# A two-layer encoder kernel: the piece of projection ahead of the scores in each attention group, and the next layer's constants loaded during the last product

## The reference, cut to what matters

```python
def encoder_trunk(x, p, ...):
    x = layer_norm(x, ln0_g, ln0_b)
    for i in range(DEPTH):                       # DEPTH = 2
        mix = hybrid_mixer(x, w_in[i], q_norm[i], k_norm[i], sink[i], ..., w_out[i], ang1d, ang2d)
        x = layer_norm(ALPHA * x + mix, ln1_g[i], ln1_b[i])
        ffn = conv_glu(x, w_up[i], conv_w[i], conv_b[i], w_down[i])
        gate = jax.nn.sigmoid(x @ w_ple_gate[i] + b_ple_gate[i])
        ple = p[i].astype(x.dtype) @ w_ple[i]
        x = layer_norm(ALPHA * x + ffn + gate * ple, ln2_g[i], ln2_b[i])
    return x

def hybrid_mixer(x, w_in, ...):
    h = x @ w_in                                 # 1024 x 1536: q, k, v of both kinds
    qa, ka, va, qb, kb, vb = jnp.split(h, ...)
    oa = global_axial_attention(...)             # 8 heads, rms-normed q and k, rotary angles
    ob = window_sink_attention(...)              # 8 heads, band of 128, a sink in the softmax
    o = jnp.concatenate([rms_norm(oa, ...), rms_norm(ob, ...)], -1)
    return o @ w_out
```

## Time and profile before

| | |
|---|---|
| median of 3 runs | 1215.49 us (1215.14 to 1216.63) |
| the profiled execution's own time | 1215.36 us |
| its span in the trace | 1213.60 us |
| granted TensorE clock, mean | 0.997 of full speed |
| busy: PE / DVE / ACT / POOL | 1192.3 / 526.7 / 492.4 / 593.9 us |
| chain of work that ended last: share on PE | 93% |
| DMA | 115.68 MB, 95 GB/s mean |

### The profile page before, as it was taken

One profiled execution on the slowest core, in us unless ns is written; L12 is line 12 of the kernel. 1 busy time (PEld: TensorE's weight loads), 2 busy tenths in 40 slices (PEclk: granted clock), 3 DMA queues, 4 the chain that ended last, 5 costly groups with the idle time before them and its releaser, 6 DMA issues.

```text
span 1213.6 us, 17810 instructions
## 1 busy us (share of the span) xinstructions
PE 1192.3 (98%) x5800; PEld 974.2 (80%) x5800; DVE 526.7 (43%) x1098; ACT 492.4 (41%) x899; POOL 593.9 (49%) x342
## 2 busy tenths in 40 slices
PE   7999999999999999999999999999999999999997
PEld 6887778888888888888878777788888888888886
DVE  7777847532122134211477777375211122431108
ACT  3456753344344333323144767433443333332321
POOL 6665844455443444344155756634653444434442
PEclk9999999999999999999999999999999999999999
DMA  6321213344333332222132202433433333222331
GB/s 220 88 74 49 88 45 113 113 130 139 98 92 87 103 104 95 79 97 95 56 90 70 80 27 70 126 116 89 139 104 104 100 90 102 90 85 91 102 104 70
DMA packets 122854, 115.68 MB, mean 95 GB/s; under 512 B 6816, under 2 KB 97952, under 8 KB 122784
## 3 DMA queue, kind: packets, MB, share of 16 engines
q1 hardware_dynamic: 122784, 114.81, 30.7%
HBM read 112.70 MB, written 2.10 MB: 95 GB/s over the span
## 4 chain that ended last, share of the span: by engine, by line
PE 93%; DVE 2%; DVEq 1%; issue 1%; POOL 1%; DMA 1%; ACT 0%; SPq 0%; ACTq 0%
PE ps L1219 28%; PE ps L1221 28%; PE ps L1220 28%; PE ps L1371 3%; PE ps L1385 3%; PE ps L1359 1%; PE ps L1361 1%; PE ps L1342 1%; PE ps L1229 1%; POOL w_lo L537 1%; DMA scratch<-in_ln_b_dram 1%; DVEq L875 0%; DVEq L1202 0%; DVE x L880 0%; POOL ln_r L533 0%
## 5 line engine op out<-in xcount | busy, mean ns | idle before, releaser
L527 POOL TENSOR_TENSOR w_lo<-raw,w_hi 128x1024 fp32r<-128x1024 f32 x192 | 461.7, 2406 | 411.4 <-ACT w_hi L635 411.4
L1219 PE MATMUL ps<-xt_hi,w_hi 128*128 128x512 f32 x704 | 273.9, 389 | 0.0
L1220 PE MATMUL ps<-xt_lo,w_hi 128*128 128x512 f32 x704 | 273.9, 389 | 0.0
L1221 PE MATMUL ps<-xt_hi,w_lo 128*128 128x512 f32 x704 | 273.9, 389 | 0.0
L635 ACT ACTIVATE w_hi<-raw 128x1024 fp32r<-128x1024 f32 x192 | 201.9, 1055 | 132.7 <-PE ps L1221 66.6
L1219 PE MATMUL ps<-w_hi,stat 128*128 128x512 f32 x480 | 188.3, 392 | 0.0
L1220 PE MATMUL ps<-w_lo,stat 128*128 128x512 f32 x480 | 187.1, 390 | 0.0
L1221 PE MATMUL ps<-w_hi,stat 128*128 128x512 f32 x480 | 187.0, 390 | 0.0
L1219 PEld LDWEIGHTS ps<-xt_hi,w_hi 128*128 128x128 f32 x704 | 132.1, 188 | 27.6
L1220 PEld LDWEIGHTS ps<-xt_lo,w_hi 128*128 128x128 f32 x704 | 132.1, 188 | 27.5
L1221 PEld LDWEIGHTS ps<-xt_hi,w_lo 128*128 128x128 f32 x704 | 132.1, 188 | 27.3
(11 more groups left out here) (123 smaller groups left out, 1330.8 us busy)
## 6 DMA issues: line engine op xcount, KB each, us to landing
raw<-in_w_up_dram SPq DMA_DIRECT2D x88, 512.0 KB, 3.8
raw<-in_w_down_dram SPq DMA_DIRECT2D x44, 512.0 KB, 3.2
raw<-in_w_in_dram SPq DMA_DIRECT2D x26, 512.0 KB, 3.8
raw<-in_w_out_dram SPq DMA_DIRECT2D x16, 512.0 KB, 3.8
raw<-in_w_ple_gate_dram SPq DMA_DIRECT2D x16, 512.0 KB, 3.9
scratch<-in_ln_g_dram SPq DMA_DIRECT2D x5, 512.0 KB, 4.5
scratch<-in_ln_b_dram SPq DMA_DIRECT2D x5, 512.0 KB, 6.0
raw<-in_w_ple_dram SPq DMA_DIRECT2D x4, 512.0 KB, 3.7
```

Of the source, the lines that this page charges most:

```text
L527: pool.tensor_tensor(w_lo[:, n, :], raw[:, n % RAW, :], w_hi[:, n, :].bitcast(F32), ALU.subtract).then_inc(w_split.sem, 1)
L1219: pe.matmul(out, a[0], b[0], start=first, stop=False)
L1220: pe.matmul(out, a[0], b[1], start=False, stop=False)
L1221: return pe.matmul(out, a[1], b[0], start=False, stop=last)
```

## The change

Five edits, all inside the layer loop or at its head:

1. In `pe_plan`, `scores(g)` for g from 2 to 31 stands behind the group's piece of projection instead of ahead of it (`scores(1)` stays).
2. `rot(2, t)` moves from g = 6, 10, 14, 18 to g = 7, 11, 15, 19, and the second `p_t` from g = 26 to g = 27, with the copies of both on ACT and DVE one group later; on DVE `mean_squares` moves from the end of its group to right behind the maxima.
3. SP loads the first layer's constants before the loop and the next layer's during the down product, behind the looped part and ahead of the last tiles; the last layer loads the first one's again.
4. DVE makes `rope_a` (`gain_tables`) before the loop and then in each layer before it waits for the down product; ACT's and DVE's waits for constants at the loop's head are gone.
5. `norm_lo(1)` at a layer's end moves behind the norm of tile 3.

```diff
@@ pe_plan
     for g in range(GROUPS + 4):
-        if 0 < g < GROUPS:
-            steps.append(("scores", g))
+        if g == 1:
+            steps.append(("scores", 1))
...
             steps.append(("ple", 0, g - 33))
+        if 1 < g < GROUPS:
+            steps.append(("scores", g))
...
-        if g in (6, 10, 14, 18):
-            steps.append(("rot", 2, (g - 6) // 4))
-        if g in (25, 26):
-            steps.append(("p_t", g - 25))
+        if g in (7, 11, 15, 19):
+            steps.append(("rot", 2, (g - 7) // 4))
+        if g in (25, 27):
+            steps.append(("p_t", (g - 25) // 2))
@@ sync
-                sp.wait_ge(h_done.sem, h_done.at(layer, 0))
...
+            load_constants(0)
...
+                following = (layer + 1) % DEPTH
+                sp.wait_ge(h_done.sem, h_done.at(layer, FT))
+                load_constants(following)
                 for r in range(1, REST):
                     raw_free(DOWN_AT + LOOPED + r)
                     load(DOWN_AT + LOOPED + r, down_source(layer, LOOPED + r), 1)
@@ vector
+            def gain_tables(landed):
+                dve.wait_ge(const_landed.sem, landed)
...
             dve.wait_ge(fixed_landed.sem, 16)
+            gain_tables(64)
             with dve.Fori(0, DEPTH) as layer:
...
-                dve.wait_ge(const_landed.sem, const_landed.at(layer, 64))
...
+                    if g in (15, 23, 31):
+                        mean_squares((g - 15) // 8)
...
+                gain_tables(const_landed.at(layer, 128))
                 for t in range(TT - 1):
                     wait_down(dve, layer, t)
                     norm_sum(t, DOWN_BANK[t], ln_rstd.at(layer, 4 + t + 1), norm_landed.at(layer, 64), down_free)
-                    if t in (1, 2):
-                        norm_lo(t - 1, xt_hi_done.at(layer, 13 + 2 * (t - 1)))
+                    if t == 1:
+                        norm_lo(0, xt_hi_done.at(layer, 13))
...
                 dve.drain().then_inc(down_free.sem, 1)
+                norm_lo(1, xt_hi_done.at(layer, 15))
```

More of the change, by code:

```diff
@@ L431, in _, with load_constants @@
             sp.dma_start(rope_sb[:, :, :, :], rope).then_inc(fixed_landed.sem, 16)
-            with sp.Fori(0, DEPTH) as layer:
-                def raw_free(s):
-                    sp.wait_ge(w_split.sem, w_split.at(layer, s - AHEAD - RAW + 1))
-                sp.wait_ge(h_done.sem, h_done.at(layer, 0))
+            def load_constants(layer):
                 sp.dma_start(cols[:, :], columns[bass.ds(layer, 1)].rearrange("a p n -> (a p) n")).then_inc(const_landed.sem, 16)
@@ L442, in _, with raw_free @@
                 sp.dma_start(sinks[:, :], bcast(sink[bass.ds(layer, 1)].rearrange("a n -> (a n)"))).then_inc(const_landed.sem, 16)
+            load_constants(0)
+            with sp.Fori(0, DEPTH) as layer:
+                def raw_free(s):
+                    sp.wait_ge(w_split.sem, w_split.at(layer, s - AHEAD - RAW + 1))
                 for s in range(AHEAD, UP_AT):
@@ L770, in _ @@
                         qkt_evac(1, 3)
-                    if g in (7, 11, 15, 19):
-                        qkt_evac(2, (g - 7) // 4)
+                    if g in (8, 12, 16, 20):
+                        qkt_evac(2, (g - 8) // 4)
                     if g in (3, 7, 11, 15):
                         win(2, (g - 3) // 4)
-                    if g in (26, 27):
-                        k = g - 26
+                    if g in (26, 28):
+                        k = (g - 26) // 2
                         act.wait_ge(tr_full.sem, tr_full.at(layer, TR["p_t", k] + 1))
@@ L909, in _ @@
                     norm_lo(t - 1, 2 * t - 1)
+            def gain_tables(landed):
+                dve.wait_ge(const_landed.sem, landed)
+                for i in range(2):
+                    g = gains[:, i, :].unsqueeze(1).to_broadcast([P, 2, HD])
+                    gs = (gains[:, i, :].rearrange("p (i b) -> p i b", b=2)[:, :, ::-1].unsqueeze(1)
+                          .to_broadcast([P, 2, HD // 2, 2]))
+                    dve.tensor_tensor(rope_a[:, 2 * i, :, :], rope_sb[:, 0, :, :], g, ALU.mult)
+                    dve.tensor_tensor(rope_a[:, 2 * i + 1, :, :].rearrange("p t (i b) -> p t i b", b=2),
+                                      rope_sb[:, 1, :, :].rearrange("p t (i b) -> p t i b", b=2), gs, ALU.mult)
+                dve.tensor_scalar(neg_sinks[:, :], sinks[:, :], -1.0, None, ALU.mult)
+                dve.drain()
+                dve.tensor_scalar(rope_a[:, 2:4, :, :], rope_a[:, 2:4, :, :], 8.0, None, ALU.mult)
+                dve.drain()
             dve.wait_ge(fixed_landed.sem, 16)
+            gain_tables(64)
             with dve.Fori(0, DEPTH) as layer:
@@ L1103, in glu @@
                     dve.tensor_tensor(dst, dst, ps[:, bank + 1, :], ALU.mult).then_inc(h_done.sem, 1)
-                dve.wait_ge(const_landed.sem, const_landed.at(layer, 64))
-                for i in range(2):
-                    g = gains[:, i, :].unsqueeze(1).to_broadcast([P, 2, HD])
-                    gs = (gains[:, i, :].rearrange("p (i b) -> p i b", b=2)[:, :, ::-1].unsqueeze(1)
-                          .to_broadcast([P, 2, HD // 2, 2]))
-                    dve.tensor_tensor(rope_a[:, 2 * i, :, :], rope_sb[:, 0, :, :], g, ALU.mult)
-                    dve.tensor_tensor(rope_a[:, 2 * i + 1, :, :].rearrange("p t (i b) -> p t i b", b=2),
-                                      rope_sb[:, 1, :, :].rearrange("p t (i b) -> p t i b", b=2), gs, ALU.mult)
-                dve.tensor_scalar(neg_sinks[:, :], sinks[:, :], -1.0, None, ALU.mult)
-                dve.drain()
-                dve.tensor_scalar(rope_a[:, 2:4, :, :], rope_a[:, 2:4, :, :], 8.0, None, ALU.mult)
-                dve.drain()
                 norm_lo(2, xt_hi_done.at(layer, 1))
@@ L1144, in _ @@
                         heads_lo((g - 6) // 2)
-                    if g in (15, 23, 31):
-                        mean_squares((g - 15) // 8)
-                    if g in (26, 27):
-                        k = g - 26
+                    if g in (26, 28):
+                        k = (g - 26) // 2
                         dve.wait_ge(p_hi.sem, p_hi.at(layer, k + 1))
```

6 lines of the change are left out of this document (3 added, 3 removed).

## The result

The changed kernel takes 1219.2 us (median of 20), the kernel before, measured beside it, 1216.3: a ratio of 1.0024 [1.0018, 1.0031]. It is slower by 0.24%, where 1215.9 and no difference were forecast; the median lies 0.2 us above the range. The forecast was counted from a median of three, 1215.49, while the 20 executions of the kernel before lie in two groups, eight from 1214.8 to 1215.5 and twelve from 1216.25 to 1216.85; so 0.8 us of the miss of 3.3 is the base, and 2.5 is the change (+0.4 forecast, +2.9 measured). The profiled execution took 1220.24 us with a span of 1218.4, so 4.88 more than the profiled execution of before.

The account below looks back on a forecast made before the run. PE, busy 98% of the span, was taken to bound the kernel. From 1215.36, +2.4 (attention), -1.2 (seam) and -0.8 (tail) give 1215.8; with the median 0.13 above, 1215.9 us, range 1211.0 to 1219.0.

Parts of the forecast that it names:

- The lead: Attention up to group 30: PE arrives there 2.8 us earlier a layer, between 1.8 and 3.4, as holes vanish.
- The new waits inside the groups: Attention groups: short new waits for DVE's rotate and ACT's later copies, put at 0.6 us, between 0 and 1.6.
- The chain: Groups 30 to 32: dependent steps to outb_half(1)'s second half take 13.18 us against 9.21, 3.97 longer.
- The step that failed: Behind groups 30 to 32: PE's dense work carries the delay through, +2.4 us for both layers (+1.2 to +4.4).
- the signs that the prediction named: Profile after: old attention holes gone, waits under 2 and about 2.5 us at outb_half, seam hole about 3, PE wait near 1.
- The seam: Between the layers: PE may go on earlier after DVE's rotate(0, 0), gain 1.2 us, bounds 2.0 and 0.
- the third rival: Seam: DVE's hole goes with the constants, gain 2.0 instead of 1.2 us, time 1215.1; chance 0.12.
- the two readings weighed: Seam: the jump's 3.19 us count from the issue of norm_lo(1)'s last operation or its end; norm_lo(2) at 620.9 to 621.5.
- The end: Last layer's tail: tile 3's norm and last store come earlier with norm_lo(1) behind, gain 0.8 us (0.5 to 1.2).
- What was to cost nothing: Down product: SP's four added constant loads (bare 1.9 us a layer) and DVE's tables (bare 1.5) are hidden in waits.
- The slower one: Attention rival: new waits in the groups eat the lead and the longer chain is paid in full, 1219.7 us; chance 0.13.
- The kept lead: Attention rival: POOL's slot 21 remainder or last outa does not bind, each layer gives 2.8, 1207.9 us; chance 0.15.

Follow-up runs that it names:

- both_links: Changed kernel with POOL making slot 21's remainder ahead of normalise(30), and outb_half(0) waiting for seven outa, outb_half(1) for the eighth: 1207.5 us.
- old_order: Changed kernel with scores(g) back ahead of the piece of projection in every group, all other edits kept: 1206.6 us.
- fill: Changed kernel with products of zeros in PE's two new waits of each layer, eight ahead of outb_half(0)'s wait, ten between outb_half(1)'s halves: 1215.4 us.
- dve_written_out: Changed kernel with scores ahead of the piece again and DVE's loop over the two layers written out as two copies: 1205.4 us.
- attention_only: Kernel before with the attention's edits alone (scores behind the piece; rot(2), p_t, mean_squares moved); constants, table, norm_lo(1) as before: 1221.8 us.
- rem21_first: Changed kernel with POOL making the remainder of slot 21 ahead of normalise(30) instead of behind it: 1211.1 us.
- s31_ahead: Changed kernel with scores(31) alone put back ahead of its piece, outb_half(0): 1210.1 us.

## Why the prediction was wrong

**The lead: right.** Forecast 2.8 us a layer. In both orders `sumsq(2)` closes group 30. PE reached it 94.45 us after the layer's first scores before and reaches it after 91.42 (160.71 - 69.29), so the lead is 3.03; with the scores ahead it is 3.28 (91.17), where 3.4 was the most that the groups could give. The new waits inside the groups were put at 0.6 and came to 0.25. The other 0.38 by which both_links is behind old_order is the wait left there.

**The chain: right.** Forecast 13.18 us from the start of group 30's piece to the second half of `outb_half(1)`. With the clock at full speed it is 171.84 - 158.70 = 13.14 in fill and 768.26 - 755.09 = 13.17 in layer 1 of after. The wait ahead of `outb_half(0)` was forecast at 1.75 and is 1.62, the other at about 2.5 and is 2.13. By waits alone the forecast was +1.2 a layer, and fill shows +0.98 and +0.97.

**The step that failed** is the sentence that closes this part: "What follows is PE's dense work, so it carries through." It carries the delay through, but not at the usual distance of starts. The pace behind a wait was taken from the earlier trace rows, where no such wait stands ahead, and each wait was weighed by its length alone. The clock's fall adds 1.55 us to a wait of 1.6 to 2.2, and it came three times in the profiled execution: +4.65 that no term and no bound held. With it the forecast's own terms give 1215.8 + 4.65 = 1220.4, and 1220.24 was measured. That this is so close is luck in part: the waits cost 0.45 less than forecast (1.95 for 2.4) and the seam gave 0.45 less (0.75 for 1.2). The upper bounds taken together, 1219.4, hold the median as well, but by a smaller lead and not by a fall. And the signs that the prediction named came out, the places and releasers of both waits, the hole ahead of `norm_lo(2)` and 0.90 us of PE's wait at the seam; none of them asks for the clock.

The trace of before had shown such a fall, at a place that the prediction does not use. At the start PE waits 2.15 us for a weight remainder, and behind it stand these two stretches:

```profile
21.77 0.50 PE L1219 MATMUL ps<-w_hi,xt_hi 128*128 128x512 f32 x1 [2.15 <-POOL w_lo L537]
```

```profile
22.00:24.00 2.00, 2.00 (x6) 1.29 (x5) 1.85 (x5) 0.00 (x0) 2.00 (x1) 0.55 0.31 87
24.00:26.00 2.00, 2.00 (x6) 1.57 (x6) 1.56 (x2) 0.34 (x1) 1.54 (x2) 0.60 0.80 210
```

There it costs next to nothing, since PE, when it is not slowed, waits again soon after: in the profiled execution of after the clock stays at the start, PE waits 0.69 us at 23.88 and 0.84 at 33.60, and the first scores are only 0.17 us earlier. At groups 32 and 33 no such slack follows. The same trace holds the other case, too: behind the 2.12 us at the seam the clock is 1.00. So the forecast could not have been certain of a fall, but it had a row for it, and its upper bound, +4.4 for both layers, should have held up to four falls more.

Single executions of the changed kernel spread from 1216.7 to 1221.6. That they differ in the number of falls would fit the size, but their mean granted clocks bear it out for the two longest at most (0.991 and 0.992); it is 0.995 at 1216.66 and at 1220.39 alike. Where this spread comes from is open.

**The seam: size off.** Forecast -1.2, measured -0.75 after, and -1.2 to -1.9 in the other kernels with all the edits of the seam and the loop as it was. The first half of the step holds, and by more than forecast: the hole behind the jump stays at 3.2 us, it did not go with the constants (the third rival), and it counts from the issue of `norm_lo(1)`. So `norm_lo(2)` starts 3.40 us after the norm of tile 3 (620.86 to 624.26), where the two readings weighed gave 4.0 and 4.6. The second half, 4.65 us from `norm_lo(2)` to the end of `rotate(0, 0)`, does not hold: the hole inside `rotate(0, 0)`, 0.46 at the seam of before, is 1.82 after and 0.46 to 1.36 in the others with the loop. A hole of 0.5 stands at the same place in layer 0 of all ten kernels with the loop, where DVE comes to it without a jump back. Here that of before:

```profile
32.23 0.70 DVE L923 TENSOR_TENSOR ps<-ps,rope_a 128x512 f32<-128x512 f32 x1 [0.49 <-issue]
```

In dve_written_out both layers are without it. So it belongs to the loop; that the part above 0.5 belongs to the jump is likely but not shown, and why its length changes from kernel to kernel is open.

**The end: right.** Forecast -0.8, measured -0.85. **What was to cost nothing** cost nothing: the stretch with the added loads and the table takes 430.19 us and took 430.16.

**The rivals.** The slower one named 1219.7, close to the time, with a mechanism that did not happen: in-group waits that eat the lead. They came to 0.25 us a layer, and none is in the list of waits. The kept lead did not happen here either, but it is what old_order and both_links do, and its 1207.9 is within 1.3 us of both.

## What to carry to other kernels

A wait of a PE-bound kernel has two prices: its length, and the pace of the products behind it. Read the granted clock by short stretches behind every wait of more than 1.5 us, the longest in the attention behind which it never fell here, and prefer several short holes to one of two; behind three holes of 0.4 to 1.5 us a layer the clock stayed before, and two of 1.6 and 2.1 cost up to 3.1 on top of their length. Where edits come in one piece, look for the order of work that the gain does not need: here the scores' order took back all that the moved transposes won.

## What the runs showed of the hardware that was not expected

A wait of two microseconds is enough for TensorE's clock to fall, and not each such wait does it. In the profiled executions it fell, in the attention, behind each of the four waits of 2.1 to 2.2 us (two in after, two in attention_only), behind two of the six of 1.62 to 1.64 us (layer 0 of after and of rem21_first) and behind neither the two of 1.50 in before nor the two of 1.0 in s31_ahead. At the start the same wait of 2.1 to 2.2 us was followed by a fall in five of the eleven kernels, before among them, and at the seam neither the 2.12 us of before nor the longest of attention_only, 2.4, by any. What decides it is open. In the attention five of the six falls came 0.4 to 1.5 us after PE was back at work, and that of layer 1 of after 0.1 before. A fall lasts for most of two rows of 2 us (in s31_ahead, at the start, for four), and in the attention each one cost 1.5 to 1.6 us. The Trainium skill, "TensorE: Matmul & The Clock Gate", section "Terms", puts the penalty at the time spent at the lower level times the share of the clock that is missing there. By the two rows of the first fall (0.50 and 0.64) that is an estimate of 2 x 0.50 + 2 x 0.36 = 1.72 us; measured was 1.55, so it holds within a tenth.

Products of zeros, which do not change what the kernel computes, kept the clock up at 1.00 in the two waits that fill put them into. And in every kernel with that loop DVE's first operation behind the loop's jump starts 3.2 to 3.5 us after `norm_lo(1)` starts, where that stands last, or after the norm of tile 3 ends, where that does.
